# Two heads at a time in the first attention of a two-block transformer kernel

## The reference, cut to what matters

```python
for blk in range(S // SB_BLOCK):            # two blocks of 128 queries
    z = einsum('bthd,bshd->bhts', qb, kb) * scale       # scores
    strict = s_idx < t_idx
    log_not = where(strict, log_sigmoid(-z), 0.0)
    suffix = cumsum(log_not, axis=3, reverse=True) - log_not
    a = where(strict, exp(log_sigmoid(z) + suffix), 0.0)
    outs.append(einsum('bhts,bshd->bthd', a, vb))       # values
...
gates = sigmoid(gate_in.reshape(B, S, 3, D))            # 3072 columns of h @ w_in
merged = gates[0] * (o_sb @ w_br_sb) + gates[1] * (o_pool @ w_br_pool) + gates[2] * (o_gm @ w_br_gm)
```

## Time and profile before

| | |
|---|---|
| median of 3 runs | 1029.85 us (1028.05 to 1029.86) |
| the profiled execution | 1031.6 us, span 1029.8 us |
| PE busy | 1013.2 us, 98% |
| DVE busy | 719.0 us, 70% |
| ACT busy | 491.5 us, 48% |
| POOL busy | 108.3 us, 11% |
| mean granted clock of PE | 0.992 |
| first attention and gate units | about 68 to 159 us of the span |

### The profile page before, as it was taken

The page is one execution under the profiler, slowest core; times in us unless marked ns, Lnnn a source line. Parts: engine busy times, 40 slices in busy tenths (PEclk is TensorE's granted clock), DMA queues, the critical chain, the costliest instruction groups (busy, mean ns, idle before and its releaser), DMA issues.

```text
span 1029.8 us, 16219 instructions
## 1 busy us (share of the span) xinstructions
PE 1013.2 (98%) x6608; PEld 889.5 (86%) x6608; DVE 719.0 (70%) x880; ACT 491.5 (48%) x559; POOL 108.3 (11%) x83
## 2 busy tenths in 40 slices
PE   8999999999999999999999999999999899999998
PEld 7997778899999888986899999887887689999996
DVE  5859657987677777854887766678776776445664
ACT  5555465554444345422554343445556665344441
POOL 1031000000110000225001000010001301000000
PEclk8999999999999998999999999999999999999999
DMA  8984345849888783596639887786551536665541
GB/s 299 371 290 137 130 142 188 287 159 345 272 300 275 265 292 116 164 293 177 219 111 346 284 280 271 261 284 209 206 183 63 170 117 212 197 203 174 194 164 42
DMA packets 119600, 223.77 MB, mean 217 GB/s; under 512 B 6575, under 2 KB 21105, under 8 KB 119537
## 3 DMA queue, kind: packets, MB, share of 16 engines
q1 hardware_dynamic: 117152, 214.97, 61.6%
q0 software_dynamic: 2256, 7.88, 2.4%
q10 hardware_dynamic: 128, 0.03, 0.0%
HBM read 217.17 MB, written 1.05 MB: 212 GB/s over the span
## 4 chain that ended last, share of the span: by engine, by line
PE 88%; DVE 6%; DMA 2%; ACT 1%; issue 1%; POOL 1%; SPq 0%; DVEq 0%; ACTq 0%; POOLq 0%
PE ps L461 83%; DMA ada_raw<-in_ada_w 2%; PE ps L817 1%; DVE lo L367 1%; PE ps L1111 1%; ACT aS L1956 1%; DMA X<-in_x 1%; DVE X L921 1%; DVE ada_acc L1134 1%; PE ps L537 1%; POOL aS L2395 1%; DVE stat L2295 1%; PE ps L950 1%; PE ps L1490 0%; PE ps L545 0%
## 5 line engine op out<-in xcount | busy, mean ns | idle before, releaser
L367 DVE TENSOR_TENSOR lo<-raw,hi 128x2048 fp32r<-128x2048 f32 x151 | 349.1, 2318 | 221.9 <-ACT hi L356 221.3
L356 ACT ACTIVATE hi<-raw 128x2048 fp32r<-128x2048 f32 x151 | 288.9, 1914 | 301.2 <-PE ps L461 272.8
L461 PE MATMUL ps<-hTh,hi 128*128 128x256 f32 x992 | 265.5, 286 | 0.3
L461 PE MATMUL ps<-hTh,lo 128*128 128x256 f32 x992 | 262.4, 283 | 0.0
L461 PE MATMUL ps<-hTl,hi 128*128 128x256 f32 x992 | 261.1, 283 | 0.0
L461 PEld LDWEIGHTS ps<-hTh,hi 128*128 128x128 f32 x992 | 182.2, 192 | 2.9 <-issue 2.4
L461 PEld LDWEIGHTS ps<-hTl,hi 128*128 128x128 f32 x992 | 181.7, 192 | 1.6 <-issue 1.2
L461 PEld LDWEIGHTS ps<-hTh,lo 128*128 128x128 f32 x992 | 182.2, 192 | 0.0
L461 PE MATMUL ps<-hi,hidh 128*128 128x512 f32 (+1 forms) x424 | 165.1, 389 | 0.0
L461 PE MATMUL ps<-hi,hidl 128*128 128x512 f32 (+1 forms) x424 | 163.6, 386 | 0.0
L461 PE MATMUL ps<-lo,hidh 128*128 128x512 f32 (+1 forms) x424 | 163.4, 385 | 0.0
(11 more groups left out here) (248 smaller groups left out, 871.1 us busy)
## 6 DMA issues: line engine op xcount, KB each, us to landing
raw<-in_mlp_w SPq DMA_DIRECT2D x64, 1024.0 KB, 5.2
ada_raw<-in_ada_w SPq DMA_DIRECT2D x44, 1024.0 KB, 7.4
raw<-in_w_in SPq DMA_DIRECT2D x20, 1024.0 KB, 7.9
raw<-in_w_ff_in SPq DMA_DIRECT2D x16, 1024.0 KB, 5.2
raw<-in_w_ff_out SPq DMA_DIRECT2D x16, 1024.0 KB, 5.3
raw<-in_attn_w_qkv SPq DMA_DIRECT2D x12, 1024.0 KB, 5.9
raw<-in_conv_w_in SPq DMA_DIRECT2D x8, 1024.0 KB, 6.3
taps<-u_pad SPq DMA_DIRECT2D x64, 71.0 KB, 6.0
```

What stands on the lines that cost most here:

```text
L356: nc.scalar.activation(hi[:, slot], raw[:, slot], ACT.Copy).then_inc(hi_made, 1)
L367: nc.vector.tensor_tensor(lo[:, slot], raw[:, slot], hi[:, slot].bitcast(F32), ALU.subtract).then_inc(lo_made, 1)
L461: return nc.tensor.matmul(o, lhs, rhs, start=start, stop=False, skip_group_check=True)
```

## The change

The heads are taken in pairs (2k, 2k + 1). Scores of both are issued behind the even unit, in the order head 0, head 1, head 0, head 1, so that neighbouring matmuls use different row halves; values of both are issued behind the next even unit, on different column halves. The first head's suffix sum is issued between the two tiles of the odd gate unit, the second's behind that unit. ACT does both softplus before the even step's split; DVE does both `log_not` before the even step's split, and both arguments before the odd step's; ACT does both exponentials before the odd step's split. The output's two parts move to the even steps.

```diff
+        def unit_x(..., tail=None, middle=lambda: None):
             for tt in range(TT):
+                if tt:
+                    middle()
...
+            def both(k):
+                return [(2 * k + i, slice(HD * i, HD * i + HD)) for i in range(2)]
-            def scores(h):
+            def scores(k):
+                if k == 0:
                     pe.wait_ge(qkv_kept, 2)
-                if h >= 2:
-                    pe.wait_ge(arg_done, h - 1)
+                else:
+                    pe.wait_ge(arg_done, 2 * k)
+                for h, r in both(k):
+                    nc.tensor.matmul(ps[:, 4 + h % 2, 0:SEQ], kT[r, k, 0:P], qT[r, k, :], ...)
+                for h, r in both(k):
+                    nc.tensor.matmul(ps[:, 4 + h % 2, SEQ:384], kT[r, k, P:SEQ], qT[r, k, P:SEQ],
+                                     ...).then_inc(z_done, 1)
             def suffix(h):                       # unchanged
                 pe.wait_ge(lnot_done, h + 1)
                 if h >= 1:
                     pe.wait_ge(arg_done, h)
...
-            def values(h):
-                pe.wait_ge(a_done, h + 1)
+            def values(k):
+                pe.wait_ge(a_done, 2 * k + 2)
+                if k:
+                    pe.wait_ge(o_lo, k)
+                for h, r in both(k):
+                    mm(pe, ps[r, 7, at:at + SEQ], vS[:, 0, ...], sbt[:, h % 2, 2, 0:SEQ], True)
+                for h, r in both(k):
+                    mm(pe, ps[r, 7, at + P:at + SEQ], vS[:, 1, ...], ...).then_inc(av_done, 1)
             for s in range(12):                  # PE
+                heads = s % 2 and s < SB_HEADS
                 unit_x(pe, U_GATE + s, ...,
+                       middle=(lambda: suffix(s - 1)) if heads else lambda: None)
-                scores(s), suffix(s - 1), values(s - 2)
+                if heads:
+                    suffix(s)
+                if s % 2 == 0 and 2 <= s < SB_HEADS + 2:
+                    values(s // 2 - 1)
+                if s % 2 == 0 and s < SB_HEADS:
+                    scores(s // 2)
             for s in range(12):                  # ACT
+                if s % 2 == 0 and s < SB_HEADS:
+                    softplus(s)
+                    softplus(s + 1)
+                if s % 2 and s < SB_HEADS:
+                    for h in (s - 1, s):
+                        act.wait_ge(arg_done, h + 1)
+                        a = sbt[:, h % 2, 2]
+                        nc.scalar.activation(a, a, ACT.Exp).then_inc(a_done, 1)
                 act_step(act, U_GATE + s)
-                softplus(s), then the exponential of head s - 1
+                if s % 2 == 0 and 2 <= s < SB_HEADS + 2:   # output's high part, was in odd steps
             for s in range(12):                  # DVE
+                if s % 2 == 0 and s < SB_HEADS:
+                    log_not(s)
+                    log_not(s + 1)
+                if s % 2 and s < SB_HEADS:
+                    argument(s - 1)
+                    argument(s)
                 dve_step(dve, U_GATE + s)
-                argument of head s - 1, then log_not(s)
                 if s == 1:
                     gating_norm()
+                if s % 2 == 0 and 2 <= s < SB_HEADS + 2:   # output's low part, was in odd steps
```

More of the change, by code:

```diff
@@ L461, in mm, with unit_x @@
             return nc.tensor.matmul(o, lhs, rhs, start=start, stop=False, skip_group_check=True)
-        def unit_x(pe, u, j, act_h, act_l, k0, outs, first, nk=4, cols=512, final=False, need=None, tail=None):
+        def unit_x(pe, u, j, act_h, act_l, k0, outs, first, nk=4, cols=512, final=False, need=None, tail=None,
+                   middle=lambda: None):
             slot = slot_of(u, j)
@@ L1481, in _ @@
             ada_sum(pe, 1)
-            def scores(h):
-                if h == 0:
+            def both(k):
+                return [(2 * k + i, slice(HD * i, HD * i + HD)) for i in range(2)]
+            def scores(k):
+                if k == 0:
                     pe.wait_ge(qkv_kept, 2)
-                if h >= 2:
-                    pe.wait_ge(arg_done, h - 1)
[L1488 to L1493, removed]
+                else:
+                    pe.wait_ge(arg_done, 2 * k)
+                for h, r in both(k):
+                    nc.tensor.matmul(ps[:, 4 + h % 2, 0:SEQ], kT[r, k, 0:P], qT[r, k, :], start=True,
+                                     stop=False, skip_group_check=True)
+                for h, r in both(k):
+                    nc.tensor.matmul(ps[:, 4 + h % 2, SEQ:384], kT[r, k, P:SEQ], qT[r, k, P:SEQ],
+                                     start=False, stop=False, skip_group_check=True).then_inc(z_done, 1)
             def suffix(h):
@@ L1503, in suffix @@
                 mm(pe, ps[:, 6, SEQ:384], tri, t[:, SEQ:384]).then_inc(sfx_done, 1)
-            def values(h):
-                pe.wait_ge(a_done, h + 1)
[L1507 to L1513, removed]
+            def values(k):
+                pe.wait_ge(a_done, 2 * k + 2)
+                if k:
+                    pe.wait_ge(o_lo, k)
+                at = (k % 2) * SEQ
+                for h, r in both(k):
+                    mm(pe, ps[r, 7, at:at + SEQ], vS[:, 0, h * HD:h * HD + HD], sbt[:, h % 2, 2, 0:SEQ], True)
+                for h, r in both(k):
+                    mm(pe, ps[r, 7, at + P:at + SEQ], vS[:, 1, h * HD:h * HD + HD],
+                       sbt[:, h % 2, 2, SEQ:384]).then_inc(av_done, 1)
             for s in range(12):
@@ L1524, in _ @@
                     pe.wait_ge(gate_kept, g - 1)
+                heads = s % 2 and s < SB_HEADS
                 unit_x(pe, U_GATE + s, None, hTh, hTl, 4 * (s % 2), lambda tt, c: ps[:, bank + tt],
[L1526 to L1532, removed]
+                       s % 2 == 0, middle=(lambda: suffix(s - 1)) if heads else lambda: None)
+                if heads:
[4 more added lines that the diff above has]
+                    scores(s // 2)
                 if s == 9:
@@ L1852, in _ @@
                     gate_from_bank(5, ACT.Sigmoid)
-                act_step(act, U_GATE + s)
[L1854 to L1862, removed]
+                if s % 2 == 0 and s < SB_HEADS:
[6 more added lines that the diff above has]
+                        nc.scalar.activation(a, a, ACT.Exp).then_inc(a_done, 1)
+                act_step(act, U_GATE + s)
+                if s % 2 == 0 and 2 <= s < SB_HEADS + 2:
+                    k = s // 2 - 1
                     act.wait_ge(av_done, 2 * k + 2)
@@ L2069, in log_not, with argument @@
                 link(dve, nc.vector.tensor_tensor(diagonals(t3), diagonals(t3), n2, ALU.add))
+            def argument(h):
+                dve.wait_ge(sfx_done, h + 1)
+                t3 = sbt[:, h % 2, 2]
+                nc.vector.tensor_tensor(t3, t3, ps[:, 6, 0:384], ALU.add).then_inc(arg_done, 1)
             for s in range(12):
-                dve_step(dve, U_GATE + s)
[L2073 to L2079, removed]
+                if s % 2 == 0 and s < SB_HEADS:
[4 more added lines that the diff above has]
+                    argument(s)
+                dve_step(dve, U_GATE + s)
                 if s == 1:
                     gating_norm()
-                if s % 2 and s >= 3 and s < SB_HEADS + 2:
-                    k = (s - 3) // 2
+                if s % 2 == 0 and 2 <= s < SB_HEADS + 2:
+                    k = s // 2 - 1
                     dve.wait_ge(o_hi, k + 1)
```

## The result

The changed kernel took 1041.08 us (median of 4 runs, 1039.42 to 1041.59), the kernel before 1029.86 us in the same series. The ratio is 1.0112 (95% interval 1.0099 to 1.0124): 11.2 us slower. The forecast was 1042.2 us, range 1035 to 1050.

The account below looks back on a forecast made before the run. TensorE (PE) bounds the kernel, 88% of the span. Some 6 us gained and some 14 us of new waits add 8.4 us to 1029.85, giving 1038.2; 4 us of slow clock makes 1042.2 us, range 1035 to 1050.

Parts of the forecast that it names:

- The deciding step: DVE's order before the second suffix sum: argument() ends at 10.71 us, PE waits from 7.75, 2.96 us in each late pair.
- The pair at the price of one head: Scores and values on PE: array halves run side by side, 0.87 and 0.81 us a pair, 1.58 us less for two heads.
- The suffix sum: On PE in each gate step: stays at 1.08 us per head, 2 x 1.08 for a pair.
- The waits: PE before the second suffix sum, four times: about 3.6, 4.3, 3.0 and 3.0 us, some 14 us in all.
- The first pair: First scores to second suffix sum: GpSimd's pooling work slows DVE, 1.0 us added, giving 11.4 us.
- the upper bound: First pair's DVE loss to GpSimd: at most 2 us, with 1.0 us taken.
- The clock: PE in the stage: slow clock behind the waits adds 4 us, bounds nothing to 13.6 us.
- The second rival: PE's clock: every one of four waits is paid with a full slow stretch, 1051.8 us or somewhat less; chance 0.13.
- the sum: First scores to pooling products: 80.97 us against 72.56, so 8.4 us added, before any clock cost.

Follow-up runs that it names:

- argument first: Changed kernel with the first head's argument() on DVE before the even step's lo split and the output's low part: 1029.32 us, ratio 1.0006 to the kernel before.
- own bank: Changed kernel with the second head's suffix sum in bank 4, no longer waiting for argument(): 1029.20 us, ratio 1.0004 to the kernel before.
- heads apart: Changed kernel with a pair's matmuls in the order head 0, head 0, head 1, head 1, for scores and values: 1041.32 us, ratio 1.0121 to before.
- own bank, gating late: Changed kernel with the second suffix sum in bank 4 and gating_norm moved from step 1 to step 7: 1021.74 us, ratio 0.9943 to before.
- filler kernel: Changed kernel with 12 unread 128-column identity matmuls on PE before the second suffix sum: 1037.48 us, ratio 1.0078 to the kernel before.

## Why the prediction was right

Its own steps, piece by piece, in us, with what the changed kernel's rows give:

| stretch | predicted | measured |
|---|---|---|
| first scores to second suffix sum | 11.4 | 12.65 |
| to the second pair's scores | 7.6 | 8.72 |
| to its second suffix sum | 12.04 | 12.01 |
| to the third pair's scores | 7.6 | 10.20 |
| to its second suffix sum | 10.71 | 10.94 |
| to the fourth pair's scores | 7.6 | 7.31 |
| to its second suffix sum | 10.71 | 10.94 |
| to the pooling products | 13.31 | 14.56 |
| sum | 80.97 | 87.33 |

- **The deciding step** was that argument() stands behind both heads' logs, the split and the low part in DVE's order. The rows show that, and two experiments that take it away at one end or the other (argument first, own bank) remove the loss.
- **The pair at the price of one head** held: 0.85 for scores and 0.80 for values. That it is the shape and not the order was shown by heads apart.
- **The suffix sum** was mis-sized: 1.08 was its price with values behind it; with a gate product behind it and the clock up it is 0.87 to 0.90 in the changed kernel. Two steps cost 14.78 instead of 15.35 where nothing waits (own bank, gating late). The kernel before has such a suffix sum too, in step 1, at 0.90:

```profile
80.92 1.14 PE L461 MATMUL ps<-sbt,cst 128*128 128x256 f32 x6
81.82 0.47 PE L461 MATMUL ps<-hi,hTh 128*128 128x512 f32 x1
```

- **The waits** sum to 15.6 instead of 13.9. In the last two pairs DVE's line is 0.23 us longer than I added up (10.94 and not 10.71). The first pair also waits 0.88 us in the middle of its odd unit, where the prediction had little or none.
- **The first pair** lost more to GpSimd than the 1.0 us that I took: L2075 and L2079 took 1.39 and 1.49 us and not 0.42, 2.0 us more than that together, the upper bound. That it is GpSimd is read from the rows, as in the kernel before; no run took GpSimd's work away.

```profile
75.23 1.39 DVE L2075 TENSOR_TENSOR sbt<-sbt,cst 128x256 f32<-128x256 f32 x1
76.79 0.56 DVE L2077 SCALAR_TENSOR_TENSOR sbt<-ps,sbt 128x384 f32<-128x384 f32 x1 [0.17 <-DVE sbt L2075]
77.38 1.49 DVE L2079 TENSOR_TENSOR sbt<-sbt,cst 128x256 f32<-128x256 f32 x1
```

- **The clock** was taken at 4 us; the filler kernel puts it at 5.5 in the profiled executions. The second rival, a full slow stretch of 6.8 us behind every wait, did not come: in the changed kernel the clock stayed at 1.00 behind the third wait, and in heads apart all four waits brought a slow stretch, but of 3.4 us. The Trainium skill ("TensorE: Matmul & The Clock Gate", on HAM oscillation) has every burst of a loop start on the slow clock when such a wait stands in each round. Heads apart agrees at all four waits, the changed kernel's trace at three of four.
- **The time itself**, 1.1 us under the forecast, is partly luck. The stage was 14.8 us longer and not 12.4, and slow stretches elsewhere, which the profiled run of the kernel before had, made up for it. The granted clocks of the single runs show what the medians hold. Seven runs of the kernel before with a mean clock of 1.000 took 1026.27 to 1026.96 us, and the one run of the filler kernel with 1.000 took 1035.17. So without slow stretches the pairs and their waits cost 8.2 to 8.9 us (the filler's own 0.45 included), where the sum had 8.4: waits 1.7 us longer than added up stand against some 0.8 us less work of PE. The forecast then put 4 us of clock on a median of the kernel before that holds slow stretches of its own: 1029.86 is 2.9 to 3.6 us above those seven runs, 1041.08 is 5.9 above the filler kernel's run, and the difference, 2.3 to 3.0 us, is what the clock added to the measured loss. These are differences between series.

## What to carry to other kernels

When work of two steps is packed into one, add up in program order what each in-order engine must do between the producer and the next consumer, unrelated splits and copies included, and compare it with the bound engine's time to that point. A buffer that two packed items share turns this sum into a wait; giving the second item its own bank (here one whose content is already read) took back the 1.1% that the change lost, and moving gating_norm as well made it a gain of 0.6%. Any block that is moved "out of the way" needs the same sum at its new place.

## What the runs showed of the hardware

- The slow clock is not a fixed price of a wait. Waits of equal length, 3.25 us, were followed by 1.2 GHz for 6.8 us, for 3.4 us, and not at all in the changed kernel's execution; in that of heads apart each of four such waits was followed by 3.4 us of it. Waits up to 2.22 us in this stage brought none in the profile of argument first. Ten of the twelve slow stretches of this stage, over all profiled executions, lasted 3.4 us, half of what the earlier trace rows show at the start of the kernel before.
- It also comes without a wait: in the kernel before PE ran 32 matmuls of one column each without a gap (397.16 to 401.5), in the midst of them, at 399.8, the clock fell to 1.2 GHz, and it stayed there for 6.8 us. The changed kernel ran the same 32 and stayed at 2.4 GHz.
- Narrow matmuls of 128 columns, whose results nobody reads, in 2.8 us of a 3.4 us wait (of 4.2 us in the first pair) were enough to hold 2.4 GHz.
- Matmuls on the two halves of rows or columns start within 0.02 us of each other whatever their order in the queue (single records of the changed kernel and of heads apart, such as 115.546 and 115.553 us, or 133.983 and 133.997): a pair costs 0.80 to 0.86 us, one head 0.79 to 0.84.
